# Merge projections of a two-layer forward pass: one ring slot for several of their units, computed piece by piece, and a new division of their sums and weight splits

## The reference, cut to what matters

```python
# first layer: three branches; gates = sigmoid(...), each (256, 1024)
y_pool = pool_mixer(...) @ w_pool_o          # 512 -> 1024
y_sb   = stick_breaking_attention(...) @ w_sb_o   # 512 -> 1024
y_x    = memory_cross_attention(...) @ w_x_o      # 256 -> 1024
merged = gates[0] * y_pool + gates[1] * y_sb + gates[2] * y_x
h = h + rmsnorm(merged @ w_out)
# then a dense feed-forward part, h = h + rmsnorm(ff)
# second layer: two branches
mixed = sigmoid(ga) * (o_a @ w_proj_a) + sigmoid(gb) * (o_b @ w_proj_b)
x = x + mixed @ w_out_2
x = x + hier_moe(rms_norm(x), ...)           # 32 experts, 6 MB of fp32 weights each
out = rms_norm(x)
```

## Time and profile before

| | us |
|---|---|
| median of 3 runs | 1137.14 |
| the profiled execution, its own time | 1136.4 |
| its span in the trace | 1134.6 |
| TensorE busy | 944.4 |
| VectorE busy | 527.2 |
| ScalarE busy | 361.9 |
| GpSimd busy | 46.4 |
| mean granted TensorE clock | 0.943 of full |

### The profile page before, as it was taken

How to read it: one execution, slowest core, us unless ns; L and a number is a source line. 1 busy time by engine, 2 the same in 40 slices (tenths; PEclk the granted TensorE clock), 3 DMA queues, 4 the chain that set the end, 5 groups by cost and what they waited for, 6 DMA issues and landing times.

```text
span 1134.6 us, 23812 instructions
## 1 busy us (share of the span) xinstructions
PE 944.4 (83%) x10517; PEld 831.3 (73%) x10517; DVE 527.2 (46%) x856; ACT 361.9 (32%) x541; POOL 46.4 (4%) x43
## 2 busy tenths in 40 slices
PE   8999999899999998999999897756565656566663
PEld 7999998899999997989988896545344534444442
DVE  4545766766655655778876742212120212121212
ACT  4544555454333335343666431100010100000001
POOL 0100001400000000000210200000000000000000
PEclk9999999999999999999999999979797978898888
DMA  9754413746555543544434988999999999999993
GB/s 338 232 186 144 150 63 115 236 134 217 184 173 200 185 156 120 171 146 155 150 120 153 356 343 362 428 425 430 429 426 430 428 426 430 428 427 429 430 427 148
DMA packets 109521, 310.03 MB, mean 273 GB/s; under 512 B 5684, under 2 KB 92408, under 8 KB 96664
## 3 DMA queue, kind: packets, MB, share of 16 engines
q1 hardware_dynamic: 107712, 304.66, 69.7%
q0 software_dynamic: 1008, 4.20, 1.0%
q10 hardware_dynamic: 744, 0.35, 0.1%
HBM read 308.14 MB, written 1.05 MB: 273 GB/s over the span
## 4 chain that ended last, share of the span: by engine, by line
PE 53%; issue 41%; DVE 3%; ACT 1%; POOL 1%; DMA 0%; ACTq 0%; POOLq 0%; DVEq 0%
PE ps L687 16%; PE ps L689 16%; PE ps L688 16%; PE ps L951 1%; DVE w_lo L1349 1%; PE ps L861 1%; PE ps L849 0%; DMA rows<-in_g_mix 0%; PE ps L790 0%; PE ps L839 0%; DVE x_f L1390 0%; PE ps L828 0%; PE ps L827 0%; DVE h L1439 0%; POOL stat L633 0%
## 5 line engine op out<-in xcount | busy, mean ns | idle before, releaser
L687 PE MATMUL ps<-x_hi,w_hi 128*128 128x256 f32 x928 | 266.3, 287 | 0.0
L688 PE MATMUL ps<-x_lo,w_hi 128*128 128x256 f32 x928 | 262.4, 283 | 0.0
L689 PE MATMUL ps<-x_hi,w_lo 128*128 128x256 f32 x928 | 262.4, 283 | 0.0
L1026 PE MATMUL ps<-arena,xg 128*32 128x128 f32 x3968 | 141.2, 305 | 68.1 <-DMA arena<-in_w 62.0
L1349 DVE TENSOR_TENSOR w_lo<-arena,w_hi 128x2048 fp32r<-128x2048 f32 (+3 forms) x83 | 166.3, 2007 | 52.8 <-ACT w_hi L1091 52.2
L1026 PEld LDWEIGHTS ps<-arena,xg 128*32 128x32 f32 x3968 | 124.5, 123 | 89.2 <-DMA arena<-in_w 77.3
L687 PEld LDWEIGHTS ps<-x_hi,w_hi 128*128 128x128 f32 x928 | 176.9, 191 | 5.4 <-issue 4.3
L688 PEld LDWEIGHTS ps<-x_lo,w_hi 128*128 128x128 f32 x928 | 177.0, 191 | 1.6 <-issue 1.0
L689 PEld LDWEIGHTS ps<-x_hi,w_lo 128*128 128x128 f32 x928 | 177.0, 191 | 0.2
L1091 ACT ACTIVATE w_hi<-arena 128x2048 fp32r<-128x2048 f32 (+3 forms) x83 | 138.6, 1671 | 40.8 <-PE ps L689 27.7
L1036 PE MATMUL ps<-arena,hid_T 128*32 128x256 f32 x992 | 75.2, 455 | 60.1 <-DMA arena<-in_w 47.3
(11 more groups left out here) (269 smaller groups left out, 1318.8 us busy)
## 6 DMA issues: line engine op xcount, KB each, us to landing
arena<-in_w SPq DMA_DIRECT2D x90, 2048.0 KB, 25.7
arena<-in_w_in SPq DMA_DIRECT2D x43, 1024.0 KB, 5.1
arena<-in_w_ffn_in SPq DMA_DIRECT2D x22, 1024.0 KB, 5.0
arena<-in_w_ffn_out SPq DMA_DIRECT2D x11, 1024.0 KB, 4.8
arena<-in_w_out SPq DMA_DIRECT2D x8, 1024.0 KB, 7.6
arena<-in_w SPq DMA_DIRECT2D x6, 1024.0 KB, 9.6
third_w<-in_w SPq DMA_DIRECT2D x3, 2048.0 KB, 12.6
arena<-in_w_mem_kv SPq DMA_DIRECT2D x2, 1024.0 KB, 5.3
```

The lines of the kernel that those rows point to most:

```text
L687: mm(dst, l_hi, r_hi, start=start, stop=False)
L688: mm(dst, l_hi, r_lo, start=False, stop=False)
L689: return mm(dst, l_lo, r_hi, start=False, stop=stop)
L1026: last = mm(ps[SLOTS * g:SLOTS * g + SLOTS, 4 + e % 2, P * n:P * n + P], xg[:, c, SLOTS * e:SLOTS * e + SLOTS], places[n][:, c, P * g:P * ...
```

## The change

It merges the projections of a branch into fewer, larger units (5 in place of 12, 4 in place of 8), each filling a ring slot, and has TensorE, VectorE and GpSimd work them off in pieces of 256 columns (numbers 0 to 11, and 12 to 19), whose banks alternate. The order of the first layer's branches becomes pool, x, sb. GpSimd adds only the x branch and the first two column groups of the last branch; the other two are added by VectorE. VectorE's splitting is suppressed at the last merge unit alone. SyncE issues the load of a unit ahead of the expert half that used to stand before it from `out20` on, and the halves of expert 0's first matrix now precede the second and the third unit of that merge.

```diff
 def unit_plan
-    for b, j in [(0, j) for j in range(4)] + [(b, j) for j in range(4) for b in (1, 2)]:
+    for b, j, n in ((0, 0, 2), (0, 2, 2), (2, 0, 4), (1, 0, 2), (1, 2, 2)):
         w, kc, o0 = branches[b]
-        add("merge", a[w][0], UC * j, kc=kc, form="B", j=j, b=b, o0=o0, last=b == 2)
+        add("merge", a[w][0], UC * j, kc=kc, cols=UC * n, form="M", js=range(j, j + n), b=b, o0=o0)
...
-        for j in range(4):
-            add("merge", a[w][0], UC * j, kc=4, form="B", j=j, b=b, o0=o0, last=b == 1)
+        for j in (0, 2):
+            add("merge", a[w][0], UC * j, kc=4, cols=2 * UC, form="M", js=range(j, j + 2), b=b, o0=o0)
 def step_plan
...
+    unit(pool01)
+    pieces(0, 1)
+    plan.append(("heads", [], [10, 11], [8, 9]))
+    plan.append(("sigmoid", 0, [(2, j) for j in range(4)]))
+    unit(pool23)
+    pieces(2, 3)
+    plan.append(("heads", [], [], [10, 11]))
+    plan.append(("sigmoid", 0, [(1, j) for j in range(4)]))
+    unit(x_all)
+    pieces(4, 5, 6, 7)
+    unit(sb01)
+    pieces(8, 9)
+    plan.append(("finish", 0))
+    unit(sb23)
+    pieces(10)
+    plan += [("finish", 1), ("finish", 2)]
+    pieces(11)
+    plan.append(("finish", 3))
...
+    a01, a23, b01, b23 = range(first["gate2"] + 8, first["gate2"] + 12)
+    unit(a01)
+    pieces(12, 13)
     plan.append(("heads", [], [26, 27], [24, 25]))
-    plan.append(("sigmoid", 1, [(1, 0)]))
-    unit(start + 1)
+    plan.append(("sigmoid", 1, [(1, 0), (1, 1)]))
+    unit(a23)
+    pieces(14, 15)
     plan.append(("heads", [], [], [26, 27]))
...
+    plan.append(("sigmoid", 1, [(1, 2), (1, 3)]))
+    unit(b01)
+    pieces(16, 17)
+    plan.append(("finish", 0))
+    unit(b23)
+    pieces(18)
+    plan += [("finish", 1), ("finish", 2)]
+    pieces(19)
+    plan.append(("finish", 3))
 SyncE
-            if u == second_merge + 2:
+            if u == second_merge + 1:
                 sp.wait_ge(o_done, 20)
                 half_load(0, 0)
-            elif u == second_merge + 3:
+            elif u == second_merge + 2:
                 half_load(0, 1)
-            elif u >= out20:
+            load(u)
+            if u >= out20:
                 if u == out20:
                     sp.wait_ge(o_done, 28)
                 which, half = divmod(u - out20, 2)
                 half_load(1 + which, half)
-            load(u)
 GpSimd
+            if layer == 0:
+                for j in range(4):
+                    add_branch(gates, 2, j, two_sum, 4 + j)
+                pool.wait_ge(two_sum, 4)
+            for j in range(2):
+                add_branch((gates, gates2)[layer], 1, j, pool_sum, (8, 16)[layer] + j)
 TensorE
+        def merge_unit(u, hi, lo):
+
+            x, m0 = units[u], piece_at[u]
+            kc, o = x["kc"], x["o0"]
+            for i in range(len(x["js"])):
+                m = m0 + i
+                if m % 12 < 2:
+                    wait_out(pe, *bank_before[u][i])
+                else:
+                    pe.wait_ge(piece_out, m - 1)
+                for nb in range(2):
+                    for c in range(kc):
+                        col = slice(UC * i + P * nb, UC * i + P * nb + P)
+                        last = three(ps[:, m % 2, T * nb:T * nb + T], hi[:, c, col], lo[:, c, col],
+                                     o_hi[:, o + c, :], o_lo[:, o + c, :], c == 0, c == kc - 1)
+                last.then_inc(piece_done if i + 1 < len(x["js"]) else unit_done, 1)
 ScalarE
-                ending = u in (out0 - 2, out0 - 1, out20 - 3, out20 - 2, out20 - 1)
-                if not ending:
+                ending = u in (out0 - 2, out0 - 1, out20 - 2, out20 - 1)
+                if u not in (out0 - 1, out20 - 1):
                     split(u + 2)
 VectorE
+        def piece(m):
+
+            u, b, j = piece_list[m]
+            g = gates if u < G0 else gates2
+            dve.wait_ge(sig_ready, (4 * (0, 2, 1)[b] if u < G0 else 12 + 4 * b) + j + 1)
+            part, total = (flat(g[:, n + 2 * j:n + 2 * j + 2, :]) for n in (8 * b, 0))
+            piece_ended(dve, m)
+            v.tensor_tensor(part, part, ps[:, m % 2, :], ALU.mult).then_inc(piece_out, 1)
+            if b == 1 and j >= 2:
+                dve.wait_ge(piece_out, m + 1)
+                if u < G0:
+                    dve.wait_ge(two_sum, j + 1)
+                v.tensor_tensor(total, total, part, ALU.add).then_inc(dve_sum, 1)
...
-                ending = u in (out0 - 2, out0 - 1, out20 - 2, out20 - 1)
-                if not ending:
+                if u not in (out0 - 1, out20 - 1):
                     split(u + 2)
...
-                if units[u]["name"] == "merge":
-                    dve.wait_ge(unit_done, u + 1)
-                    merge(u)
-                    if ending:
-                        split(u + 1)
```

More of the change, by code:

```diff
@@ L196, in step_plan, with pieces @@
     plan.append(("sigmoid", 0, [(0, j) for j in range(4)]))
-    start = first["merge"]
-    for n in range(12):
-        unit(start + n)
-        if n == 0:
-            plan.append(("heads", [], [10, 11], [8, 9]))
-        elif n == 1:
-            plan.append(("heads", [], [], [10, 11]))
-        if n < 4:
-            plan.append(("sigmoid", 0, [(1, n), (2, n)]))
-        if n in (6, 8):
-            plan.append(("finish", n // 2 - 3))
-    plan += [("finish", 2), ("finish", 3)]
+    pool01, pool23, x_all, sb01, sb23 = range(first["merge"], first["merge"] + 5)
+    def pieces(*ms):
+        plan.extend(("piece", m) for m in ms)
+    unit(pool01)
[16 more added lines that the diff above has]
+    plan.append(("finish", 3))
     for u in range(first["out"], first["out"] + 4):
@@ L477, in outs, with wait_out @@
     def outs(u, vector):
-        return sum((x["name"] in BY_VECTOR) == vector for x in units[:u + 1] if x["form"] != "F")
-    def wait_out(eng, u):
-        if units[u]["name"] in BY_VECTOR:
+        return sum((x["name"] in BY_VECTOR) == vector for x in units[:u + 1]
+                   if x["form"] != "F" and x["name"] not in BY_HALF + ("merge",))
+    def wait_out(eng, u, half=1):
+        if units[u]["name"] == "merge":
+            eng.wait_ge(piece_out, piece_at[u] + len(units[u]["js"]) - 1 + half)
+        elif units[u]["name"] in BY_VECTOR:
             eng.wait_ge(out_dve, outs(u, True))
@@ L506, in layers_kernel, with piece_ended @@
     second_merge = first["gate2"] + 8
+    def piece_ended(eng, m):
+        u = piece_list[m][0]
+        if m + 1 < len(piece_list) and piece_list[m + 1][0] == u:
+            eng.wait_ge(piece_done, m + 1 - sum(v < u for v in piece_at))
+        else:
+            eng.wait_ge(unit_done, u + 1)
     N_ROPE = len(rope_of)
@@ L698, in unit @@
                 return down(x["i"], hi, lo)
-            if bank_before[u] is not None:
-                wait_out(pe, bank_before[u])
+            if x["form"] == "M":
+                return merge_unit(u, hi, lo)
+            for before in bank_before[u]:
+                if before is not None:
+                    wait_out(pe, *before)
             part_ready = None
@@ L897, in _ @@
                 u = arg[0]
-                if units[u]["name"] == "merge" and units[u]["j"] == 0:
+                if units[u]["name"] == "merge":
                     if units[u]["b"] == 0:
@@ L974, in _ @@
                     row(1)
-            elif step in ("finish", "topk", "select", "sigmoid"):
+            elif step in ("piece", "finish", "topk", "select", "sigmoid"):
                 pass
@@ L1235, in _ @@
                     evacuate(u)
-                if u == out20 - 1:
-                    split(out20)
                 if (u + 3 < G0 or u >= G0 + 3 * NF) and not ending:
```

72 lines of the change are left out of this document (34 added, 38 removed).

## The result

| | runs | median, us | lowest to highest | profiled execution (span) |
|---|---|---|---|---|
| before | 6 | 1137.02 | 1136.28 to 1137.66 | 1136.4 (1134.6) |
| after | 6 | 1130.35 | 1127.77 to 1133.92 | 1127.77 (1126.0) |

The ratio is 0.9937, 95% interval 0.9922 to 0.9952: 6.7 us less. The prediction's 1128.5 was 1.9 too low, inside its range. Its profiled execution was put at 1127.8 and took 1127.77.

The account below looks back on a forecast made before the run. TensorE and its issue were taken to bound the kernel up to the experts, then a DMA stream that ends a fixed time after starting. Gains of 4.0 and 4.6 sum to 8.6, taking the median from 1137.14 to 1128.5 us; range 1125.6 to 1133.1.

Parts of the forecast that it names:

- The first merge: Sum of terms up to the end of `out0`, put at 216.8 against 220.8: 4.0 us gained.
- 1.05 for `o_lo`: New TensorE wait ahead of branch x, and again branch b, for VectorE's two copies of the last head values: 1.05 us.
- The allowance of 0.1: First merge: 0.1 us allowed for VectorE's 2.3 us split standing ahead of piece 4.
- the clock's 1.7: Time lost to a granted clock of 0.75 over 6.7 us behind each long gap: 1.7 us in each merge, to be regained.
- The 1.3 us of room: First merge: slack for `finish` 1, due on VectorE at 208.4 ahead of piece 11's multiply, before GpSimd's adds delay `out0`.
- The second merge: Sum of terms at `out20`, including new waits of 1.05 for `o_lo` and 0.65 for group 3: 4.6 us gained.
- SyncE's queue: Second merge: 7 MB queued from 622.8; `out21` lands about 632, `out22` 637, `out23` 643, with no room left but nothing lost.
- A: Rival, chance 0.07: the stream is short of DMA and the second merge's gain is lost, giving 1133.1 us.
- B: Rival, chance 0.04: one queue's transfers don't land in order, `out21` lands near 642, gain 2.8, time 1134.3 us.
- C: Rival, chance 0.10: the four short new gaps cost the clock 1.7 us each; two give 1131.9, all four 1135.3.
- D: Rival, chance 0.05: slower, GpSimd's adds block VectorE's in-order queue; 1135.5 us at 3.20 per add, 1139.4 at 3.9.
- what follows keeps its intervals: Assumption that everything behind `out0` and `out20` keeps its timing, so the 8.6 us gained there reaches the end.

Follow-up runs that it names:

- before_again: The kernel before, unchanged, profiled and run once more: median 1137.76 us in 11 runs.
- e9: After, with GpSimd adding all four column groups of each merge and VectorE none: median 1136.12 us, ratio to before 0.9993.
- e5: After, with the last head pair's values computed one piece sooner (between pieces 2 and 3, and 14 and 15): median 1133.07 us.
- e2: Before, its units kept, with only the splits of `out0` and `out20` made sooner: median 1137.08 us, ratio to before 0.9998.
- e4: After, with short ones-matmuls filling three new gaps and the wait inside `out20`: median 1131.32 us, ratio to before 0.9937.
- e1: After again, unchanged: median 1131.87 us in 9 runs, ratio to before 0.9946; with after's first 6 runs, 15 runs with median 1131.75.
- e3: After, with VectorE's splits of `out0` and `out20` put back behind the last multiply: median 1141.26 us, ratio to before 1.0026.
- e7: After, with expert 4's loads waiting for expert 1's end in place of expert 2's: median 1132.06 us.

## Why the prediction was right

**The first merge** was put at 4.0 us and gave 4.02 (220.81 to 216.79). Each term was found: 0.3 for piece 2's bank (0.37), 1.05 for `o_lo` (1.01), 0.75 for piece 11's multiply (0.90), nothing for the split of `out0`, clock 1.00, no second wait for group 3 (`x_lo` ends at 212.8, wanted at 213.0). The allowance of 0.1 was not needed. That the sum fits to 0.02 is luck all the same. With the clock's 1.7 measured at 1.53 (the 48 matmuls took 7.51 us and now 5.98) these terms give 3.73; the merge began 0.17 later; and 0.46 came from what the prediction didn't have, less time outside the waits (from the first merge matmul to `out0` 33.04 us, now 32.58). Against before_again, whose clock fell longer, the gain would have been 5.2.

The prediction also named the wrong instruction ahead of piece 11's multiply. It is `finish` 2, not `finish` 1: its `x_lo` ends at 209.9, as piece 11 does, and the multiply starts at 209.98. The 1.3 us of room that it counted for `finish` 1 were none for `finish` 2. It came out without a loss because VectorE's own add feeds it, which is what e9 took away. e5 shows how thin the cover ahead of it was: VectorE's split did collide with x's pieces as soon as TensorE came 1 us earlier.

**The second merge** was put at 4.6. `out20`'s 48 matmuls end at 638.46 in place of 647.06, 8.6, of which 4.08 came from ahead of it: 4.5. Here too 1.05 was 1.01, and 0.65 for `x_lo` was 0.82. By e2, 2.4 of the 4.5 come with the sooner split alone. SyncE's chain held: expert 2 was put at 8.6 sooner and left 8.60 sooner, expert 3 at 676.40 as said.

**SyncE's queue.** ScalarE split `out21` and `out22` from 633.73 with no wait and waited 2.00 us for `out23`, landed at 639.4, which was put at 643: nothing on TensorE's path. A and B fall: the weights landed in time for readers that want them in order.

**C** falls for gaps of up to 1.03: in every profile whose gap ahead of `out0` is no longer, the clock behind it was 1.00, and e4's fillers changed nothing. e9 gives both sides: behind 1.75 in `out0` it was 1.00, behind 2.29 in `out20` 0.84; and in e2, behind 2.47, it was 0.83 from 210 to 220. The rows of before had only 0.88 and 2.98.

**D** did not happen, but its mechanism is real, and it is the change's own adds on VectorE that keep it away. I priced these adds as a step of 0.69 in group 3's chain and left open what GpSimd in their place would cost. e9 says 4.2 us in the profile and 4.4 in the median (1136.12 against the 1131.75 of 15 runs). Their worth is more than the difference of two durations: `finish` 2 would stand ahead of piece 11's multiply, and the wait would reach the length that costs the clock.

**What failed** is the sentence that what follows keeps its intervals. It held in the profiled execution to 0.1 us (464.1 behind expert 2 in both) and not in the median: 6.7 of 8.6 arrived, 6 over 15 runs. I took the intervals from one profile and three runs; later series of before went up to 1142.3. The profiles show four places where an execution can lose time: the stage behind the FFN (2.2 us), the fillers at the lower clock (1.6 us on expert 3's load, e1), code that arrives late (0.5 to 3.2 us in the sum, by the time from expert 3's load to the tail), and the tail (1.3 to 4.0). All but the stalls were seen on before's units as well (e2). The profiles can't say which of them makes up the missing 2 us: both of after's own are faster than its median, and both of before's own are without any of the four. Why only after's code was seen to stall stays open.

## What to carry to other kernels

A split or load that is made sooner is worth something only if its buffer is free sooner and nothing urgent stands behind it in its engine's queue: here the larger units alone gave nothing (e3) and the sooner split alone nothing in one merge and 2.4 us in the other (e2), together 8.6 us. When a short wait is removed, look at what it had covered (e5), and at which engine feeds the instruction ahead of the urgent one in an in-order queue (e9). A gain ahead of a transfer-bound stage should be checked over some ten runs, since clock and code loading may take part of it back, and a profile of one run should be cut into stages before two profiles are compared: in e2 a gain in one stage was hidden by a loss in another.

## What the runs showed of the hardware

Packets of 16 KB of the kind instruction run during the execution, 44 of them in after, and beside a full data queue TensorE stood for 1.2 to 2.7 us in the middle of a run of equal matmuls, in e1 around such a packet. The profile puts this down to issue. The place stays the same from kernel to kernel and moves by as many instructions as the code ahead of it gains or loses (58 to 55 of 128 with 6 more, 91 to 103 with 6 fillers fewer).

The granted clock kept 1.00 behind gaps of 0.82 to 1.03 us in `out0` and `out20`, and behind one of 1.75 in e9; it fell to 0.84 over 11 us behind one of 2.29. Behind the FFN the same code with the same gaps (1.34 and 1.52 us ahead of the stretch, in after and in e7) had 1.00 in seven profiles of eleven with after's merges and about 0.85 in four, from 440 to 455. Behind the same wait of 3.2 us 48 matmuls took 7.5 us in one profile of before and 8.6 in the other.
